# A hybrid decoder step on one core: marks of the last block from preloaded numbers, scatter indices copied early, two output tiles by plain stores, eight first weight tiles

## The reference, cut to what matters

```python
x = layer_norm(ALPHA * x + mix, ln1_g[l], ln1_b[l])
ffn = hier_moe(x, w_group[l], b_group[l], w_router[l], b_router[l],
               w_gate[l], w_up[l], w_down[l])
x = layer_norm(ALPHA * x + ffn, ln2_g[l], ln2_b[l])
...
h = jax.nn.silu(jnp.einsum('td,edf->tef', xf, w_gate)) * jnp.einsum('td,edf->tef', xf, w_up)
y = jnp.einsum('tef,te,efd->td', h, gate.astype(h.dtype), w_down)
```

## Time and profile before

| | us |
|---|---|
| median of 3 runs | 1553.38 |
| the profiled execution | 1553.51 |
| its span | 1551.7 |
| PE busy | 1475.0 (95%) |
| DVE busy | 986.0 (64%) |
| ACT busy | 750.6 (48%) |
| POOL busy | 166.0 (11%) |
| chain that ended last: PE / DVE / DMA | 84% / 9% / 4% |
| mean granted TensorE clock | 0.97 |

### The profile page before, as it was taken

One profiled execution on the slowest core, in us unless ns is written; L12 is line 12 of the kernel. 1 busy time (PEld: TensorE's weight loads), 2 busy tenths in 40 slices (PEclk: granted clock), 3 DMA queues, 4 the chain that ended last, 5 costly groups with the idle time before them and its releaser, 6 DMA issues.

```text
span 1551.7 us, 24068 instructions
## 1 busy us (share of the span) xinstructions
PE 1475.0 (95%) x9374; PEld 1299.7 (84%) x9374; DVE 986.0 (64%) x1221; ACT 750.6 (48%) x869; POOL 166.0 (11%) x93
## 2 busy tenths in 40 slices
PE   8999999999999999999997789999999999999984
PEld 7998898889999989999997348888888888888771
DVE  4234525436768687721224738888888888888766
ACT  4224333324424433411110037777788887777655
POOL 0000000000000000134340001111111112111010
PEclk9999999999999999999998789999999999999997
DMA  7321321132313122534424399999999999999996
GB/s 268 106 82 55 101 91 59 55 104 74 111 55 111 65 74 98 163 130 150 164 83 183 109 386 388 380 391 384 392 372 385 391 393 394 379 382 385 342 294 147
DMA packets 89354, 336.46 MB, mean 217 GB/s; under 512 B 11821, under 2 KB 18629, under 8 KB 60273
## 3 DMA queue, kind: packets, MB, share of 16 engines
q1 hardware_dynamic: 84095, 315.59, 54.6%
q0 software_dynamic: 5184, 19.79, 5.2%
HBM read 314.67 MB, written 41.78 MB: 230 GB/s over the span
## 4 chain that ended last, share of the span: by engine, by line
PE 84%; DVE 9%; DMA 4%; issue 1%; ACT 1%; SPq 0%; DVEq 0%; ACTq 0%
PE BANK L1635 13%; PE BANK L1636 12%; PE BANK L1637 12%; PE BANK L1981 6%; PE BANK L1983 6%; PE BANK L1982 6%; PE BANK L2018 4%; PE BANK L2020 4%; PE BANK L2019 4%; DMA RAWB<-in_w_up 3%; PE BANK L1965 2%; PE BANK L1994 2%; PE BANK L1697 2%; PE BANK L1720 2%; PE BANK L1776 2%; PE BANK L1653 1%
## 5 line engine op out<-in xcount | busy, mean ns | idle before, releaser
L1512 DVE TENSOR_TENSOR LOB<-RAWB,HIB 128x2048 fp32r<-128x2048 f32 x196 | 448.8, 2292 | 97.5 <-ACT HIB L950 96.9
L1635 PE MATMUL BANK<-XH,HI 128*128 128x260 f32 x1746 | 507.0, 290 | 1.6 <-DVE RT L1337 1.0
L1636 PE MATMUL BANK<-XL,HI 128*128 128x260 f32 x1746 | 496.6, 284 | 0.0
L1637 PE MATMUL BANK<-XH,LO 128*128 128x260 f32 x1746 | 496.2, 284 | 0.0
L950 ACT ACTIVATE HIB<-RAWB 128x2048 fp32r<-128x2048 f32 x196 | 376.3, 1920 | 131.4 <-PE BANK L1983 67.8
L1635 PEld LDWEIGHTS BANK<-XH,HI 128*128 128x128 f32 x1746 | 332.8, 191 | 18.1 <-issue 17.3
L1636 PEld LDWEIGHTS BANK<-XL,HI 128*128 128x128 f32 x1746 | 332.7, 191 | 0.0
L1637 PEld LDWEIGHTS BANK<-XH,LO 128*128 128x128 f32 x1746 | 332.5, 190 | 0.0
L1981 PE MATMUL BANK<-HIB,XGH 128*128 128x512 f32 x512 | 202.8, 396 | 6.3 <-issue 3.0
L1983 PE MATMUL BANK<-LOB,XGH 128*128 128x512 f32 x512 | 200.9, 392 | 0.0
L1982 PE MATMUL BANK<-HIB,XGL 128*128 128x512 f32 x512 | 200.8, 392 | 0.0
(11 more groups left out here) (344 smaller groups left out, 1571.8 us busy)
## 6 DMA issues: line engine op xcount, KB each, us to landing
RAWB<-in_w_gate SPq DMA_DIRECT2D x68, 1024.0 KB, 9.8
RAWB<-in_w_up SPq DMA_DIRECT2D x68, 1024.0 KB, 10.8
RAWB<-in_w_down SPq DMA_DIRECT2D x68, 1024.0 KB, 11.6
RAW<-in_w_in SPq DMA_DIRECT2D x39, 1024.0 KB, 4.9
RAW<-in_w_out SPq DMA_DIRECT2D x16, 1024.0 KB, 5.5
Y<-in_xT SPq DMA_DIRECT2D x8, 520.0 KB, 9.2
RT<-in_xT SPq DMA_DIRECT2D x16, 260.0 KB, 5.9
x_rows<-R SPq DMA_DIRECT2D x5, 832.0 KB
```

The lines of the kernel that those rows point to most:

```text
L1512: dve.tensor_tensor(LOB[:, s, :], RAWB[:, r, :], HIB[:, s, :].bitcast(F32), ALU.subtract).then_inc(b_lo[s], 1)
L1635: pe.matmul(bank, hw[:, c, :], h, start=(c == 0), stop=False)
L1636: pe.matmul(bank, hw[:, c, :], l, start=False, stop=False)
L1637: ins = pe.matmul(bank, lw[:, c, :], h, start=False, stop=(c == KC - 1))
```

## The change

- **First blocks.** Two more raw places `RAW67` are laid over the middle places of `HIB` and `LOB`. All 8 tiles of block 0 are loaded before the router's result (tiles 6 and 7 right behind the last part of `p_rows`). A tile of block 1 waits for one used tile less by two (`b_used >= i + 1`), and `s` is `i % NRAW` everywhere. Parts 3 and 4 of `x1_rows` are stored behind the first tile of block 1, the `y_set` stores move two tiles back.
- **Marks.** `IOS` (the numbers) gets 128 partitions and is loaded with the router's constants; `COUNT` and its two DMAs go. DVE makes `blo(3)` ahead of `TOKF` and the marks, and no longer waits for `f_ln` there but, for 96, ahead of the first `centred`. PE waits for the marks by `f_add`.
- **Scatter.** The index copy stands ahead of the wait for `b_y`, behind a new wait for the scatter before (`b_yw >= 16 * j`).
- **Output.** `NACC = 2`: only tiles 0 and 1 go through ACT's scaling and the accumulating DMA; tiles 2 and 3 are finished by DVE (`finished`, a pass with `LB2`) and stored plainly by SP. `YA` now covers raw places 0 to 3, `LG2` and `LB2` places 4 and 5. ACT takes `mean(0)` ahead of the four sample copies.

```diff
-    LG2 = sb("LG2", [128, D], F32, O_RING)
-    LB2 = sb("LB2", [128, D], F32, O_RING + 8192)
-    YA = sb("YA", [128, NF, D], F32, O_RING + 16384)
+    LG2 = sb("LG2", [128, D], F32, O_RING + 32768)
+    LB2 = sb("LB2", [128, D], F32, O_RING + 40960)
+    YA = sb("YA", [128, NF, D], F32, O_RING)
+    RAW67 = [sb(f"RAW{6 + k}", [128, 2048], F32, O_RING + 49152 + 8192 + 24576 * k) for k in range(2)]
...
-                s = (2 + i) % NRAW if m0 is not None else i % NRAW
+                s = i % NRAW
                 if m0 is None:
-                    if i >= NRAW:
-                        sp.wait_ge(b_used, i - NRAW + 1)
-                elif isinstance(j, int) and i < NRAW:
-                    sp.wait_ge(b_used, 3 + i)
+                    sp.dma_start(first_tile(i), w).then_inc(b_raw[s] if i < NRAW else s_wr, 16)
+                    return
+                if isinstance(j, int) and i < NRAW:
+                    sp.wait_ge(b_used, i + 1)
...
             sp.dma_start(p_out[:, :, 1920:2048], R[:, :, 1920:2048]).then_inc(s_x1w, 16)
+            for i in range(NRAW, 8):
+                bload(i, None, ...)
...
-            for i in range(1, NT):
+            for i in range(1, 3):
                 x1_out(i)
-            for i in range(NRAW, 8):
-                bload(i, None, ...)
...
-                    if isinstance(j, int) and 1 <= i <= NT:
-                        y_set(i - 1)
+                    if isinstance(j, int) and i == 1:
+                        x1_out(3)
+                        x1_out(4)
+                    if isinstance(j, int) and 3 <= i < 3 + NT:
+                        y_set(i - 3)
...
-            sp.dma_start(COUNT[0:TT, :], a["ios"]).then_inc(f_ln, 16)
-            sp.dma_start(COUNT[TT:128, :], a["ios"][0:128 - TT, :]).then_inc(f_ln, 16)
...
+            for i in range(NACC, NF):
+                sp.wait_ge(f_y, i + 1)
+                sp.dma_start(o["yp"][128 * i:128 * i + 128, :], YA[:, i, :]).then_inc(f_out, 16)
             sp.wait_ge(f_y, NF + 1)
-            sp.dma_start(o["yp"][128 * (NF - 1):128 * NF, :], YA[:, NF - 1, :]).then_inc(f_out, 16)
-            sp.wait_ge(f_y, NF + 2)
...
             def scatter(j):
-                pool.wait_ge(b_y, 4 * j + 2)
+                pool.wait_ge(b_yw, 16 * j)
                 passed(pool)
                 pool.tensor_copy(YIXC[:, :], YIX[:, bass.ds(j - 1, 1)]).then_inc(b_iy, 1)
                 pool.wait_ge(b_iy, j)
+                passed(pool)
+                pool.wait_ge(b_y, 4 * j + 2)
                 passed(pool)
...
-            samples_copy(0)
-            samples_copy(1)
             mean(0)
-            samples_copy(2)
-            samples_copy(3)
+            for n in range(4):
+                samples_copy(n)
...
-            scaled(2)
...
+            blo(3, 0, nb)
             done(dve.tensor_copy(TOKF[:, :], YIX[:, bass.ds(last, 1)]))
-            dve.wait_ge(f_ln, 16 * 8)
             for i in range(NF):
-                ts(OWN[:, i, :], COUNT[:, :], float(CAP + 128 * i), TOKF[:, 0:1], ALU.add, ALU.is_equal)
-            ts(OWN8[:, :], COUNT[:, 0:DB], float(CAP + SEQ), TOKF[:, 0:1], ALU.add, ALU.is_equal)
-            blo(3, 0, nb)
+                ts(OWN[:, i, :], IOS[:, :], float(CAP + 128 * i), TOKF[:, 0:1], ALU.add, ALU.is_equal)
+            ts(OWN8[:, :], IOS[:, 0:DB], float(CAP + SEQ), TOKF[:, 0:1], ALU.add, ALU.is_equal).then_inc(f_add, 1)
...
+            def finished(i):
+                root(i, None)
+                dve.scalar_tensor_tensor(YA[:, i, :], YA[:, i, :], MV2[:, i, 2:3], LB2[:, :], ALU.mult, ALU.add).then_inc(f_y, 1)
 
             added(0)
+            dve.wait_ge(f_ln, 96)
             centred(0)
...
             centred(2)
-            root(2)
+            finished(2)
             centred(3)
-            root(3)
-            dve.scalar_tensor_tensor(YA[:, 3, :], YA[:, 3, :], MV2[:, 3, 2:3], LB2[:, :], ALU.mult, ALU.add).then_inc(f_y, 1)
+            finished(3)
...
+            pe.wait_ge(f_add, 1)
             for n in range(4):
                 pe.wait_ge(b_y, 4 * nb - 1 + n)
```

More of the change, by code:

```diff
@@ L213, in build @@
     W8 = sb("W8", [128, 2, 64], F32, O_8 + 1024)
-    COUNT = sb("COUNT", [128, 128], F32, O_8 + 3072)
     OWN8 = sb("OWN8", [128, DB], F32, O_8 + 3584)
@@ L317, in build @@
         s_lg = sem("ln1_in")
-        s_wr = sem("router_in")
+        s_wr = sem("router_and_two_tiles_in")
         s_var = sem("ln_var")
@@ L369, in build @@
         f_p = sem("last_rows_spread")
-        f_add = sem("last_rows_added")
+        f_add = sem("last_rows_marked_and_added")
         f_sc = sem("y_scaled")
         TRI = small("TRI", [TT, TT])
-        IOS = small("IOS", [TT, 128])
+        IOS = small("IOS", [128, 128])
         SLOT = small("SLOT", [TT, 128])
@@ L442, in last_bank, with first_tile @@
             return ((0, 1, 2, 3), (6, 7, 4, 5))[k % 2][n]
+        def first_tile(i):
+            return RAWB[:, i, :] if i < NRAW else RAW67[i - NRAW][:, :]
         def slot(u):
@@ L580, in _ @@
                     sp.dma_start(LG[:, :], a["ln1g"]).then_inc(s_lg, 16)
-                    for t, s in ((TRI, "tri"), (IOS, "ios"), (THB, "thb"), (IO24, "io24"), (IO4, "io4"), (IO16, "io16"), (CUTS, "cuts"), (VAL, "val"), (LIM, "lim"), (RB, "rb")):
+                    for t, s in ((TRI, "tri"), (THB, "thb"), (IO24, "io24"), (IO4, "io4"), (IO16, "io16"), (CUTS, "cuts"), (VAL, "val"), (LIM, "lim"), (RB, "rb")):
                         sp.dma_start(t[:], a[s]).then_inc(s_rc, 16)
@@ L584, in _ @@
                     i = (n - 5) // 2
-                    if i < NF - 1:
+                    if i < NACC:
                         sp.dma_start(o["yp"][128 * i:128 * i + 64, :], a["ln2b"][0:64, :]).then_inc(f_out, 16)
                         sp.dma_start(o["yp"][128 * i + 64:128 * i + 128, :], a["ln2b"][0:64, :]).then_inc(f_out, 16)
+                if n == 0:
+                    sp.dma_start(IOS[0:TT, :], a["ios"]).then_inc(s_rc, 16)
+                    sp.dma_start(IOS[TT:128, :], a["ios"][0:128 - TT, :]).then_inc(s_rc, 16)
                 if n == 2:
@@ L746, in _ @@
             passed(pool)
-            pool.wait_ge(f_out, 32 * (NF - 1))
-            for i in range(NF - 1):
+            pool.wait_ge(f_out, 32 * NACC)
+            for i in range(NACC):
                 pool.wait_ge(f_sc, i + 1)
                 pool.dma_start(out=o["yp"][128 * i:128 * i + 128, :], in_=YA[:, i, :], accum_op=ALU.add).then_inc(b_yw, 16)
-            pool.wait_ge(b_yw, 16 * nb + 16 * (NF - 1))
+            pool.wait_ge(b_yw, 16 * nb + 16 * NACC)
             passed(pool)
@@ L945, in bhi @@
             def bhi(i, m0, j):
-                s, r = (2 + i) % NHL, (2 + i) % NRAW
-                act.wait_ge(b_raw[r], 16 * ((8 + i) // NRAW + 1) + 32 * (j - 1))
+                s, r = (2 + i) % NHL, i % NRAW
+                act.wait_ge(b_raw[r], 16 * (2 + i // NRAW) + 32 * (j - 1))
                 if not isinstance(j, int) or i >= 2:
@@ L1352, in _ @@
                 if n == 6:
-                    dve.wait_ge(s_rc, 160)
+                    dve.wait_ge(s_rc, 176)
                     v = VAL[:, :, :, :].rearrange("p c i k -> p (c i) k")
@@ L1915, in _ @@
             pe.wait_ge(r_hot, 1)
-            pe.wait_ge(s_rc, 160)
+            pe.wait_ge(s_rc, 176)
             hot = RK[:, :, :].rearrange("p i e -> p (i e)")
@@ L1989, in first_gate_up @@
                 for i in range(8):
[L1990 to L1991 removed]
+                    pe.wait_ge(b_raw[i] if i < NRAW else s_wr, 16 if i < NRAW else 64)
+                    w = first_tile(i).rearrange("p (c n) -> p c n", c=4)
                     for c in range(4):
```

25 lines of the change are left out of this document (12 added, 13 removed).

## The result

The changed kernel has a median of 1539.91 us (1536.54 to 1542.58, 4 runs) against 1553.1 us for the kernel before on the same chip (1552.52 to 1553.41, 4 runs): a ratio of 0.9914, 95% interval 0.9893 to 0.9936, so 13.2 us faster, with 10 to 17 inside the interval. The profiled execution took 1536.54 us, its span is 1534.7 us. A second set of runs of the unchanged text gave 1539.87 us (1538.18 to 1543.69, 7 runs). The forecast was 1537.0, range 1533.0 to 1542.5.

What follows compares the result with a forecast made beforehand. PE and the DMA engines are both full in the loop, so changes at its two ends shift the end one for one. Front 7.3 plus back 9.1 is 16.4 us off 1553.51, predicting 1537.0 us, range 1533.0 to 1542.5.

Steps and rivals of the forecast that it cites:

- Step 1: Front: tiles 6 and 7 of block 0 load into idle DMA engines, taking 5 us of work off the full stretch.
- Steps 2 and 3: Front: block 1's second tile lands at 908.2; silu, its table load hidden, starts 5.5 us earlier, at about 911.05.
- Rival A: Front: the gather for block 1 becomes the wait, price 2 to 4 us, giving 1540; chance 0.12.
- step 5: Front: half clock at block 1's start costs 2.0 us; gain between 0 and 2.0, taken as 0.6.
- Step 4: Front: PE's 1.12 us stop in block 1 goes with its restart, gaining 1.2 us, bound 0.
- rivals C and D: Loop: C, DMAs bound it, head start lost, 1544.4, chance 0.06; D, earlier scatter and gather stop PE, slower, 0.03.
- Step 6: Back: `blo(3)` no longer waits, PE runs the last down tile at full clock; owners' rows start 6.7 us earlier.
- Step 7: Back: scatter starts at 1494.4 instead of 1496.42, `X2` 0 to 2.0 us earlier; at most 0.5 us felt.
- Step 9: Back: DVE gets one more pass of 2.35 us for tile 2, fully on its path.
- Step 10: Back: accumulating stores move 205 GB/s, loads 422; with fewer, the DMAs' end moves from about 1549.4 to 1540.3.
- Rival B: End: stores still limit it, back gains 6 us (1540), or 4.05 (1542) if the fourth pass alone counts; chance 0.13.

Runs made afterwards that it cites:

- rows first: The changed kernel with parts 3 and 4 of `x1_rows` stored ahead of block 1's first tile: 1539.22 us, ratio 0.990.
- late `y_rows`: The changed kernel with one `y_rows` store behind tile 6 of block 1 and one behind each down tile: 1543.26 us, ratio 0.9937.
- front alone: The kernel before with only the edits of the first blocks: 1550.9 us, ratio 0.9972.
- spread constants: The changed kernel with `LG2` and `LB2` loaded into even and odd partitions instead of lower and upper 64: 1538.05 us, again 1538.68 us.
- three accumulations: The changed kernel with tile 2 again scaled on ACT and stored by accumulation, without DVE's extra pass: 1543.56 us, ratio 0.9934.
- both orders: The changed kernel with `x1_rows` parts 3 and 4 ahead of block 1's first tile and `y_rows` stores behind tile 6 and the down tiles: 1541.79 us.

## Why the prediction was right, and where it was not

The sum was 16.4 us; counted from the router it is 13.8 to 15.3 in the profiles and 13.2 in the medians. The range held the time, and the back was right in size; the front gave half of what was forecast, which the range was wide enough to hold. Point by point:

- **Step 1** (tiles 6 and 7 early) is confirmed: 406 GB/s at 856 us, where nothing moved.
- **Steps 2 and 3** (silu 5.5 us earlier, table load hidden) are right to the tenth: silu starts 0.04 us behind block 0's end, against 5.57 before. (The second tile landed earlier than step 2 says, at 62.0 us from the router's start where its 908.2 is 66.6; nothing hung on it.)
- **Rival A** (chance 0.12) came true beside the forecast, a little under its price: 1.48 and 1.99 us on PE against 2 to 4. Block 1 still begins 4.9 and 3.9 us earlier. I had weighed the missing tiles 6 and 7 against two parts behind a tile. With these parts behind the tile the gather is issued 3.6 us later, counted from the router (60.5 against 56.9), and its landing took 10.3 and 10.6 us against 9.6; with rows first it is issued at 56.5. Rows first shows that without this wait block 1 begins 6.5 us earlier, so the half clock did give back about 1 us, step 5, in the turn itself.
- **Step 4** (the 1.12 us stop goes, 1.2 us gained) is the one that failed. The stop at tile 5 did go, but one of 2.00 us came at tile 7, and 3.4 us at half clock behind it cost another 1.7, where before the half clock had lain at block 1's beginning and cost 2.0, step 5. So block 1 lasted 39.0 us from its first product to its turned `H`, against 38.3: a loss of 0.7. With no stop and no half clock, in the run with late `y_rows`, it lasted 34.8. The working looked at tile 5 alone and counted both the earlier issue and the queue shorter by 5 us. But the engines were full or nearly full from 892 us on, and there the 9.8 us of earlier issue brought tile 7 in only 5.3 us earlier, about what the 2 MB taken off the queue are worth, while PE wanted it 7.9 us earlier. The bound given, 0, should have been a loss. The late `y_rows` stores show that it is the backlog: with fewer bytes ahead of tile 7 the stop in block 1 is gone, and comes later. Where PE itself is late, because the half clock slowed block 1's beginning for 10.2 us (front alone, and the second profile with spread constants), the stop was gone too and `H` was turned at 114.05 and 114.47 us; with the full clock at first and the stop it was 114.8 to 115.9.
- Together the front gave 3 to 4 us where 7.3 were forecast.
- **Loop, rivals C and D**: the period is 35.15 us. The front's gain at block 1, 4.2 and 3.2 us, is still there in the last pass, 4.0 and 3.3. At the loop's exit PE idles for 3.0 us in every kernel, before and after; the half clock around it lasts 0, 3.4 or 6.8 us (none in the first profile after, 3.4 before and in the second one, 6.8 in the front alone). The two profiles of the changed text differ in it, and from the last pass to the last `H` it takes 31.0, 32.6 or 33.7 us.
- **Step 6** forecast 6.7 us for the owners' products; from the last `H` it is 23.70 us before and 16.82 after: 6.9. PE runs the last down tile without a stop, at full clock.
- **Step 7** was mis-sized. The scatter is issued earlier, but the `X2` loads are not: counted from the last `H` they go out after 17.4 and 16.8 us, against 16.8 before, where up to 2 us earlier was forecast. The owners' products have moved 6.9 us forward, so DVE is free for `X2` well before it lands. DVE's first add comes 4.8 to 5.4 us behind the owners' products, against 1.1 before. The list closes its gaps, and 0.9 to 1.4 us of that is felt (the last `H` to DVE's end is 50.4 and 49.9 us, where the steps give 53.5 - 6.9 + 2.35 = 49.0), where at most 0.5 was allowed. With spread constants it is 48.7 in both profiles: nothing is felt.
- **Step 9** (+2.35 us) is confirmed by three accumulations: without the pass, 2.2 and 1.7 us less than in the two profiles of the change.
- **Step 10**: the last store lands 3.7 us behind its issue, against 8.5 before; 3 to 4 was the forecast. The span then ends 6.6 to 6.9 us nearer to DVE's end than before, with 1.8 us that I had not counted: before, 2.2 us passed between the last landing and the span's end, now 0.4, and with three accumulations 2.5 again. What fills them I did not find out. The accumulations at about 205 GB/s, where plain stores move 400, explain the rest. Had an accumulation cost no more than a plain store, three of them would have ended the kernel about 2 us before two, by the pass that DVE saves; they end it 5.0 to 5.8 us later. The Trainium skill ("DMA: Bandwidth & Descriptors", the anatomy of one DMA) gives for a DMA issued by GpSimd, as the accumulating ones are, about 2 us and its bytes at 436 GB/s; here they moved 205 to 221 GB/s with full engines, so the measurement decides against that figure for them. Rival B is out: the back gained more than its 6 or 4 us.
- **Back together**: 9.7 and 10.5 us from the last `H` to the end, 9.1 forecast, within its bounds of 6.5 to 10.5.

So the total is 2.9 us off in the medians: an error of 3 to 4 us at the front, less about 1 us by which the back was put too low.

## What to carry to other kernels

When the engines that move data are already full, cost a transfer by the bytes ahead of it, not by its issue: here an issue 9.8 us earlier landed 5.3 us earlier. Then ask when each later transfer is wanted, not only the one that is late now, for the stop may move there. When you take a wait away, look at what was late beside it; here the scatter and `X2` took over at once. Look at what full DMA engines move, not only at how busy they are: 234 and 205 GB/s at a full busy share, where 400 was possible, pointed both at the accumulating stores and at the constants.

## What was not expected of the hardware

- Loads of 512 KB into 64 neighbouring partitions moved 225 to 236 GB/s with full engines; the same bytes to every second partition 418 to 434.
- A gap of PE of 2 to 3 us was followed, beginning between one microsecond before its end and two behind it, by a stretch of 3.4 or 6.8 us at a granted clock of 0.50 (1.2 GHz), in some executions and not in others: none behind the 3.00 us at the loop's exit in the first profile after, none behind the 2.34 us with both orders. At the loop's exit 3.4 us of it cost 1.6 us and 6.8 us cost 2.7. In the profiles the router's start lies between 839.2 and 845.9 us, about as far apart as most runs of one kernel; whether such stretches in the projections make all of that was not counted. Here is one, from about 203.6 to 206.8 us of the kernel with rows first:

```profile
200.00:204.00 4.00, 4.00 (x50) 3.85 (x49) 0.00 (x0) 1.47 (x4) 0.00 (x0) 0.96 0.00 0
204.00:208.00 4.00, 4.00 (x24) 3.97 (x24) 0.71 (x3) 0.89 (x1) 0.00 (x0) 0.61 0.00 0
```

PE is busy for 4.00 of 4.00 us in both, so its busy time does not show the loss; in PE's timeline the large matmuls (L1644 to L1646) follow each other at 0.22 us in the stretch and at 0.12 us outside it. The counts can't be compared, as the first window holds many small matmuls of another line.
